# Feed-forward down product in 2x2 blocks with seven products, up product in sixteen steps

## The reference

```python
    hn = rmsnorm_2(h, norm2_g[layer])
    a = jnp.square(jax.nn.relu(hn @ w_ff1[layer].astype(f32)))
    h = h + a @ w_ff2[layer].astype(f32)
```

## Time and profile before

| | us |
|---|---|
| median of 3 runs | 760.32 (760.21 to 760.4) |
| profiled execution | 762.41 |
| its span, first to last instruction | 760.6 |
| TensorE busy in the span | 685.4 (90%) |
| VectorE busy | 366.6 (48%) |
| ScalarE busy | 290.9 (38%) |

### The profile page before, as it was taken

How to read it: one execution, slowest core, us unless ns; L and a number is a source line. 1 busy time by engine, 2 the same in 40 slices (tenths; PEclk the granted TensorE clock), 3 DMA queues, 4 the chain that set the end, 5 groups by cost and what they waited for, 6 DMA issues and landing times.

```text
span 760.6 us, 12999 instructions
## 1 busy us (share of the span) xinstructions
PE 685.4 (90%) x5446; PEld 535.4 (70%) x5446; DVE 366.6 (48%) x585; ACT 290.9 (38%) x426; POOL 48.8 (6%) x84
## 2 busy tenths in 40 slices
PE   3999989899767577667999999999999999999996
PEld 2887878753322232222999989999989999998895
DVE  3568861422100000103876987544875744565453
ACT  4235430241110110003757452667456553344532
POOL 0000000000000000000039660000000000000000
PEclk9999999989988897889999999999999999999999
DMA  8999899999999999999944634430645445564001
GB/s 354 402 415 404 312 422 420 423 380 424 422 424 420 427 420 426 411 417 414 400 157 179 223 113 150 184 111 2 222 168 192 180 159 215 221 219 168 2 1 55
DMA packets 33038, 210.27 MB, mean 276 GB/s; under 512 B 4688, under 2 KB 5072, under 8 KB 8656
## 3 DMA queue, kind: packets, MB, share of 16 engines
q1 hardware_dynamic: 32976, 209.38, 69.0%
HBM read 208.32 MB, written 1.05 MB: 275 GB/s over the span
## 4 chain that ended last, share of the span: by engine, by line
PE 70%; DMA 22%; DVE 3%; ACT 2%; SPq 1%; issue 1%; DVEq 0%
PE psum L421 69%; DMA raw<-in_w_exp 17%; DMA raw<-in_w_in_t 3%; PE psum L429 1%; SPq L476 1%; DMA raw<-in_w_in 1%; DMA raw<-in_w_ada_q 1%; ACT whi L497 0%; DVE X L2476 0%; DVE wlo L514 0%; DVE acc L536 0%; ACT XT L2423 0%; ACT Sp L840 0%; DVE gates L2085 0%; ACT MH L1854 0%
## 5 line engine op out<-in xcount | busy, mean ns | idle before, releaser
L421 PE MATMUL psum<-XH,whi 128*128 128x256 f32 x736 | 210.6, 286 | 3.5 <-DVE XL L667 2.6
L421 PE MATMUL psum<-XH,wlo 128*128 128x256 f32 x736 | 208.4, 283 | 0.0
L421 PE MATMUL psum<-XL,whi 128*128 128x256 f32 x736 | 208.1, 283 | 0.0
L514 DVE TENSOR_TENSOR wlo<-raw,whi 128x2048 fp32r<-128x2048 f32 (+1 forms) x88 | 169.0, 1959 | 35.8 <-ACT whi L497 35.8
L497 ACT ACTIVATE whi<-raw 128x2048 fp32r<-128x2048 f32 (+1 forms) x79 | 139.4, 1802 | 55.8 <-PE psum L421 37.2
L421 PEld LDWEIGHTS psum<-XH,whi 128*128 128x128 f32 x736 | 139.2, 189 | 8.0 <-issue 4.0
L421 PEld LDWEIGHTS psum<-XL,whi 128*128 128x128 f32 x736 | 138.8, 189 | 0.3
L421 PEld LDWEIGHTS psum<-XH,wlo 128*128 128x128 f32 x736 | 139.0, 189 | 0.0
L421 PE MATMUL psum<-raw,G 128*32 128x512 f32 x456 | 67.5, 674 | 19.7 <-DMA raw<-in_w_exp 19.7
L421 PEld LDWEIGHTS psum<-raw,G 128*32 128x32 f32 x456 | 18.1, 122 | 55.8 <-issue 54.8
L421 PE MATMUL psum<-raw,XT 128*32 128x512 f32 x248 | 38.0, 748 | 20.1 <-DMA raw<-in_w_exp 18.8
(11 more groups left out here) (351 smaller groups left out, 951.7 us busy)
## 6 DMA issues: line engine op xcount, KB each, us to landing
raw<-in_w_exp SPq DMA_DIRECT2D x85, 1024.0 KB, 23.1
raw<-in_w_ff SPq DMA_DIRECT2D x32, 1024.0 KB, 5.3
raw<-in_w_in SPq DMA_DIRECT2D x22, 1024.0 KB, 7.4
raw<-in_w_ada SPq DMA_DIRECT2D x16, 1024.0 KB, 12.0
raw<-in_w_in_t SPq DMA_DIRECT2D x8, 1024.0 KB, 18.2
X<-in_w_exp SPq DMA_DIRECT2D x5, 1024.0 KB, 24.6
raw<-in_w_ada_q SPq DMA_DIRECT2D x4, 1024.0 KB, 17.5
raw<-in_w_out_t SPq DMA_DIRECT2D x4, 1024.0 KB, 9.9
```

The lines of the kernel that those rows point to most:

```text
L421: return e.matmul(o, l, r, start=start, stop=stop, skip_group_check=True)
L514: e.tensor_tensor(wlo[j % NS][:, x], ring[slot[i]][:, x], whi[j % NS][:, x], ALU.subtract).then_inc(*steps_(("lo", j, x.start // 1024), *[ ...
```

## The change

The 4096 hidden features are now taken in sixteen steps of 256. For step p, the squared relu is a 2 x 2 block matrix: A11, A12 are its two feature blocks of 128 for the first 128 tokens, A21, A22 the same for the last 128. The piece of `w_ff2` is a 2 x 2 block matrix of 128 x 512 blocks B. In eleven of the sixteen steps the four output blocks are made from seven block products (Winograd's form of Strassen's scheme) that add up over the steps in seven PSUM banks P1 to P7:

- P1 = A11 B11, P2 = A12 B21, P3 = S4 B22, P4 = A22 T4, P5 = S1 B12, P6 = S2 T2, P7 = S3 T3
- S1 = A21 + A22, S3 = A11 - A21, S2 = S1 - A11, S4 = A12 - S2
- T3 = B22 - B12, T2 = B22 - (B12 - B11), T4 = B21 - T2

The outputs are formed once at the end. In the five steps named `PLAIN` (3, 7, 11, 14, 15) eight products are made, into P2 to P5. VectorE makes the sums of both kinds; ScalarE and VectorE split them into high and low halves like everything else, so per step 896 columns of activations and, of the sums, 1536 of weights. The square moves from VectorE to ScalarE. The up product of a step (48 matmuls of 256 columns) has one PSUM bank for all steps but one, since seven banks are taken; it waits for the relu of the step before. TensorE's order is up 0, 1, 2, pair 0, up 3, pair 1, and so on. The ring has five buffers from here on (buffers 0 and 6 hold the split weights of the odd pairs), and `w_ff1`, `w_ff2` are laid out by step.

```diff
@@ the pieces
-        for j in range(9):
-            if j < 8:
-                pieces += [("w", a["w_ff1_2"], j, k) for k in range(2)]
-            if j:
-                pieces += [("w", a["w_ff2_2"], b, j - 1) for b in range(2)]
+        pieces += [("w", a["w_ff1_2"], h, 0) for h in range(4)] + [("w", a["w_ff2_2"], p, 0) for p in range(2)]
+        for h in range(4, 16):
+            pieces += [("w", a["w_ff1_2"], h, 0), ("w", a["w_ff2_2"], h - 2, 0)]
+        pieces += [("w", a["w_ff2_2"], p, 0) for p in range(14, 16)]
...
+            elif i >= F0:
+                k = 1 + (i - F0) % (NR - 2)
...
@@ ScalarE
+            for h in range(16):
+                if h == 0 or 3 <= h < 15:
+                    act_down_high(e, h - 1 if h else 1)
+                if h == 15:
+                    act_down_high(e, 14)
+                    act_down_high(e, 15)
+                act_up(e, h)
+                if 2 <= h < 14:
+                    act_up_high(e, h + 2)
+                if h == 1:
+                    act_down_high(e, 0)
+                act_blocks(e, h)
...
+        def act_up(e, h):
+            e.wait_ge(*at(("up", h)))
...
+            for n in range(2):
+                e.activation(up_blocks(h, n), up_bank(h)[:, 256 * n:256 * n + 256].rearrange("p (a b) -> p a b", a=2),
+                             ACT.Relu).then_inc(*ff_act(("relu", h)))
...
+        def act_down_high(e, p):
...
+            e.wait_ge(*landed(f2(p)) if p in PLAIN else at(("sums", p)))
+            e.activation(down_at(p)[0][:, :], ring[slot[f2(p)]], ACT.Copy).then_inc(*ff_act(("down_high", p)))
+            if p not in PLAIN:
+                e.activation(down_at(p)[2][:, 0:1536], TM[p % 2], ACT.Copy).then_inc(*ff_act(("down_high_sums", p)))
...
@@ VectorE
+            dve_down_sums(e, 1)
+            dve_down_sums(e, 0)
+            for h in range(16):
+                if h == 0 or 3 <= h < 15:
+                    dve_down_low(e, h - 1 if h else 1)
+                if h >= 2:
+                    dve_down_sums(e, h)
...
+                dve_blocks(e, h)
+                if 2 <= h < 14:
+                    dve_up_low(e, h + 2)
+                if h == 1:
+                    dve_down_low(e, 0)
+                dve_blocks_low(e, h)
...
@@ TensorE
+            for h in range(16):
...
+                pe_up(e, h)
+                if h == 2:
...
+                    e.wait_ge(*at(("relu", 1)))
+                if h >= 2 and h - 2 in PLAIN:
+                    pe_plain(e, h - 2)
+                elif h >= 2:
+                    pe_seven(e, h - 2)
+            pe_down_last(e)
+
+        def pe_up(e, h):
+            if h >= 2:
+                e.wait_ge(*at(("relu", h - 1 if h > 2 else 0)))
...
+        def pe_seven(e, p):
+            H, L, (h, l, h3, l3) = FH[p % 4], FL[p % 4], down_at(p)
+            e.wait_ge(*at(("F", p)))
+            e.wait_ge(*at(("down_low", p)))
+            for o, x, w in ((P1, A11, B11), (P2, A12, B21), (P3, SA4, B22), (P5, SA1, B12)):
+                mm3(e, o[:, :], (H[:, x, :], L[:, x, :]), (h[:, w], l[:, w]), p == 0, False)
+            e.wait_ge(*at(("down_low_sums", p)))
...
```

More of the change, by code:

```diff
@@ L122, in build @@
         ps = [psum[:, 512 * i:512 * i + 512] for i in range(8)]
-        raw = [sb(f"raw{i}", [128, 2048]) for i in range(NR)]
+        fh, fl = ExitStack(), ExitStack()
+        oddH = tensors(fh)("oddH", [128, 2048], fr)
+        fh.close()
+        raw = [sb(f"raw{i}", [128, 2048]) for i in range(NR - 1)]
+        oddL = tensors(fl)("oddL", [128, 2048], fr)
+        fl.close()
+        raw.append(sb(f"raw{NR - 1}", [128, 2048]))
         halves = ExitStack()
@@ L140, in build @@
         both.close()
-        raw += [sb(f"raw{NR + 2 * NS + i}", [128, 2048]) for i in range(2)]
+        HL = NR + 2 * NS
+        raw += [sb(f"raw{HL + i}", [128, 2048]) for i in range(2)]
         XT = sb("XT", [128, 8, 256])
@@ L2395, in act_ff @@
                 e.wait_ge(*at(n))
[L2396 to L2409, removed]
+            for h in range(16):
[10 more added lines that the diff above has]
+                act_blocks(e, h)
+            e.wait_ge(*at(("pair", 13)))
+            e.activation(V, P6[:, :], ACT.Copy).then_inc(*ff_act("v"))
+            act_part(e, 1, slice(0, 512), ("x4", 1, 0), ss[:, 1:2])
             act_part(e, 0, slice(0, 512), ("x4", 0, 0), ss[:, 0:1])
@@ new lines, in act_blocks, with act_up_high @@
+        def act_blocks(e, p):
+            n = 6 if p in PLAIN else 7
+            e.wait_ge(*at(("blocks", p)))
+            if p >= 4:
+                e.wait_ge(*at(("pair", p - 4)))
+            e.activation(flat(FH[p % 4][:, 0:n, :]), flat(AB[p % 2][:, 0:n, :]), ACT.Copy).then_inc(*ff_act(("FH", p)))
+        def act_up_high(e, h):
+            i = f1(h)
+            e.wait_ge(*landed(i))
+            e.wait_ge(*at(("up", h - 2)))
+            e.activation(whi[f1_at(h)][:, :], ring[slot[i]], ACT.Copy).then_inc(*ff_act(("up_high", h)))
@@ L2438, in dve_ff @@
                 e.wait_ge(*at(n))
[L2439 to L2450, removed]
@@ new lines, in dve_ff @@
+            lo, hi = slice(0, 512), slice(512, 1024)
+            e.wait_ge(*at(("pair", 13)))
+            for t in range(2):
+                e.wait_ge(*at(("x3_rq", t)))
+            dve_add(e, 0, hi, P1[:, :])
+            e.wait_ge(*at("v"))
+            e.tensor_tensor(V, V, P1[:, :], ALU.add).then_inc(*ff_dve())
+            e.wait_ge(*ff_dve.last())
+            e.tensor_tensor(U3, V, P7[:, :], ALU.add).then_inc(*ff_dve())
+            dve_add(e, 0, lo, V)
+            e.wait_ge(*ff_dve.last())
@@ L2476, in dve_sum, with dve_down_sums @@
             e.scalar_tensor_tensor(out=X[:, t, cs], in0=p, scalar=rq[:, t:t + 1], in1=X[:, t, cs], op0=ALU.mult, op1=ALU.add).then_inc(
-                *ff_dve(("x4", t, part)))
+                *ff_dve(*[name] if name else []))
+        def dve_down_sums(e, p):
+            if p in PLAIN:
+                return
+            r, m = ring[slot[f2(p)]], TM[p % 2]
+            before = [q for q in range(p % 2, p, 2) if q not in PLAIN]
+            if before:
+                e.wait_ge(*at(("down_low_sums", before[-1])))
+            e.wait_ge(*landed(f2(p)))
+            e.tensor_tensor(m[:, T3], r[:, B22], r[:, B12], ALU.subtract).then_inc(*ff_dve())
+            e.wait_ge(*ff_dve.last())
+            e.tensor_tensor(r[:, B12], r[:, B12], r[:, B11], ALU.subtract).then_inc(*ff_dve())
+            e.wait_ge(*ff_dve.last())
+            e.tensor_tensor(m[:, T2], r[:, B22], r[:, B12], ALU.subtract).then_inc(*ff_dve())
+            e.wait_ge(*ff_dve.last())
+            e.tensor_tensor(m[:, T4], r[:, B21], m[:, T2], ALU.subtract).then_inc(*ff_dve(("sums", p)))
@@ L2484, in pe_ff @@
         def pe_ff(e):
[L2485 to L2490, removed]
+            for h in range(16):
+                if h < 2 and (7, 6)[h] in holder:
+                    e.wait_ge(*at(("read", holder[(7, 6)[h]])))
+                pe_up(e, h)
+                if h == 2:
+                    for k in range(6):
@@ L2491, in pe_ff @@
                         if k in holder:
                             e.wait_ge(*at(("read", holder[k])))
[L2493 to L2509, removed]
@@ new lines, in pe_plain @@
+        def pe_plain(e, p):
+            H, L, (h, l, h3, l3) = FH[p % 4], FL[p % 4], down_at(p)
+            e.wait_ge(*at(("F", p)))
+            e.wait_ge(*at(("down_low", p)))
+            for o, x, y in ((P5, (A21_, A22_), (B12, B22)), (P3, (D1, D2), (B12, B22)),
+                            (P2, (A11, A12), (B11, B21)), (P4, (A21_, A22_), (B11, B21))):
+                for k in range(2):
+                    i = mm3(e, o[:, :], (H[:, x[k], :], L[:, x[k], :]), (h[:, y[k]], l[:, y[k]]), False, False)
+            i.then_inc(*ff_pe(("pair", p)))
```

153 lines of the change are left out of this document (129 added, 24 removed).

## The result

The changed kernel takes **764.35 us** (median of 4 runs, 764.16 to 764.59), the kernel before 760.36 in the same comparison (4 runs, 760.21 to 761.68): ratio 1.0045, interval 1.0033 to 1.0057. By the medians it is 4.0 us slower, by the ratio 3.4 (interval 2.5 to 4.3), although TensorE has 33 matmuls fewer.

A forecast was written before the change was run, and what follows sets the result against it. TensorE's matmuls were taken to bound the stage; -7.48 + 6.85 + 2.1 + 1.1 = +2.6 us on the median 760.32 gave 762.9, own range 761.9 to 764.2, 8 in 10 range 758.4 to 765.6.

The forecast's parts named there:

- 33 matmuls less: TensorE over the stage: eleven pairs each drop three 512-column matmuls of 0.2267 us, -7.48 us.
- two waits: Opening: TensorE waits 2.3 us before the third up product and 4.5 before pair 0; taken as +6.85 us.
- slow clock: Behind the second wait: TensorE at 1.2 GHz for a stretch, +2.1 us, the mean of eight earlier gaps (1.38 to 2.94).
- tail: End of the stage: last scaling ends 4.50 us past TensorE's end instead of 3.40, +1.1 us (bounds 0.5 and 2).
- The term without spread: TensorE's saving from 33 fewer 512-column matmuls, -7.48 us, given without any range.
- my bound between gaps with and without the slow clock: Idle gaps in the expert stage: 3.14 us was followed by full clock, those from 3.46 us by 1.2 GHz.
- with the clock unharmed: Opening: the waits come but the clock stays full; +0.5 us, 760.8, no change; chance 0.20.
- with a shorter opening: Opening: one of the two waits is covered, without the second no slow clock; -4.1 us, 756.2; chance 0.18.
- The steady state at nothing: Middle steps: VectorE needs 38.5 us per three seven-product pairs and a plain one, TensorE 42.76; priced at 0.
- The loads: Five-buffer ring: down pieces requested about 14 us ahead of their sums, landing takes 5.3 us; cost 0.

The follow-up runs named there:

- both waits filled: Changed kernel plus 18 unread 512-column matmuls ahead of pair 0 and 10 ahead of up 2: 761.91 us, ratio 1.0018.
- the second experiment: Changed kernel with pair 0 ahead of pair 1 on VectorE and ScalarE, and relus of up 0 and 1 moved earlier: 755.41 us, ratio 0.9942.
- the relu first: Changed kernel with ScalarE doing the relu and square of up 0 ahead of the high half of pair 1: 764.11 us, ratio 1.0048.
- the tail alone: Changed kernel with VectorE's scaling of the first 128 tokens moved behind the addition of P4: 762.4 us, ratio 1.0027.

## Why the prediction was right

The forecast of 762.9 was slower than before and missed by 1.5 us. The measured 764.35 lies in the range for 8 in 10 (758.4 to 765.6), but 0.15 above the forecast's own range (761.9 to 764.2). Luck did not make it: the two terms that were clearly off, the matmuls and the clock, both made the forecast too low and did not cancel. Term by term:

| term | predicted | measured | from |
|---|---|---|---|
| 33 matmuls less | -7.48 | -7.48 + 0.5 | see below |
| two waits | +6.85 (computed 2.3 + 4.5) | +6.76 | 2.46 + 4.30 |
| slow clock | +2.1 | +2.7 (2.9 by the window) | both waits filled |
| tail | +1.1 | +1.02 | 4.54 - 3.52 |
| sum | +2.6 | +3.5; the trace has 2.70 + 1.02 = +3.7 | medians +4.0, ratio +3.4 |

**The matmuls.** 5446 became 5413 on the page, and 339 matmuls of 512 columns are in the stage (61 + 52 triples). The term without spread did have one. The kernel with plain pairs at the start has no wait and 27 matmuls less than before, 6.12 us, yet its stage is 746.53 - 572.15 = 174.38, only 5.59 shorter. About 0.5 us is missing. In that kernel 331 successive 512-column matmuls follow each other after 0.2287 us on average, 0.2275 in the kernel before: 0.4 us over 339. The changed kernel at full clock has 0.2288 (312 of them), so the longer distance is not that one kernel's; why it is longer was not tested. The prediction's 0.2267, from three matmuls in a row, was a little low for the kernel before too.

**The opening.** Both waits were found where the order put them, with the releasers named ahead: 2.46 us for ScalarE's relu (predicted 2.3) and 4.30 for VectorE's low half of pair 0 (predicted 4.5). That another order alone removes them is shown by the second experiment. The step was right.

**The clock.** The mechanism was right: with the waits filled the clock stayed at 1.00 and the time came back. Its size, +2.1, was the mean of eight earlier gaps and is the term most mis-sized; the changed kernel's profile lies near the upper bound of 2.94, while two others with pair 0 at the same distance lost only 1.6, so that within these bounds the size is partly chance. And my bound between gaps with and without the slow clock, 3.14 to 3.46 us from the earlier trace rows, does not hold here: 2.57 us was enough in two profiles. The rivals with the clock unharmed (760.8) and with a shorter opening (756.2) both fell in this kernel; the second is what the reordered opening then did on purpose.

The Trainium skill, "TensorE: Matmul & The Clock Gate" (part 1, "What's actually happening"), which I had set beside this term, has the half-rate clock as the default that activity releases; the filled waits agree with it.

**The steady state at nothing.** Right: TensorE is busy 100.00 of 100 us in the middle, and VectorE 89.8%, where the prediction's 38.5 of 42.76 us is 90%. The margin was real but thin: with three more seven-product pairs it is gone. The loads landed in 4.9 us at the median, and no wait of TensorE in the stage was released by one.

**The tail.** Right in place and size: P4's addition stood behind the scaling, as computed, and moving the scaling took 1.35 us off.

## What to carry to other kernels

When a change takes work from the bounding engine and gives it to the others, cost the first step by hand, with each engine's instructions in its own order: eleven savings of 0.68 us were lost to one delay of 6.8 us, and a new order turned +0.45% into -0.6% (with the tail -0.9%). Ask of each early instruction who waits behind it, and put what the bounding engine wants first ahead of what only will be wanted. How many products to replace is set by the other engine: with eleven of sixteen VectorE was busy 90% and TensorE never waited for it in the middle, with fourteen it was busy 95% and TensorE waited at nearly every step.

## What I had not expected of the hardware

- An idle gap of 2.57 us was followed by a stretch at 1.2 GHz in two profiles, one of 2.46 us in the changed kernel was not. By the times, one kernel does it in some executions only: with one wait filled, three of seven runs lie near 764.1 and four near 761.8.
- What such a stretch costs depends on where it falls. With the same start of pair 0, 24.9 us into the stage, it cost 2.7 us in one profile and 1.6 in two others. In the first (the changed kernel) the clock had been low for 1.1 us when TensorE started again. In the second (the relu first) it had been low for 2.9 us at least (line below), so less of the stretch was left to fall on matmuls. In the third (the tail alone) half of it fell on up 2, in front of another wait, and cost nothing.
- Where the clock was already low at the restart, the first 512-column matmul was longer (0.77 us in the changed kernel and with the relu first) than its neighbours at the same clock (0.63). With the tail alone, where the clock was still full just ahead of the restart, it was 0.61.

```profile
595.00:597.88 2.88, 0.01 (x1) 0.04 (x1) 2.44 (x2) 2.88 (x5) 0.00 (x0) 0.50 0.00 0
```

This is the window just ahead of that kernel's restart at 597.88: TensorE idle, its granted clock already 0.50.
